# The causal mask of all attention scores moves from TensorE products to a VectorE addition in PSUM

## The chip, the core and the metric

The kernel runs on one core of a Trainium2 chip. Its time is the device time of one execution in microseconds (us). The engines are named as in the profile: PE is TensorE (PEld its weight loads), DVE is VectorE, ACT is ScalarE, POOL is GpSimd, SP is the engine that issues DMAs. PSUM (`ps` in the rows, 8 banks of 512 float32 columns on 128 partitions) is where TensorE writes its products; VectorE and ScalarE read it.

## What is computed

Two layers of a hybrid decoder over 512 positions of width 1024: a projection, three groups of token mixers (gated delta rule, sparse attention, short convolution), an output projection, and a gated FFN. The change touches the attention group alone, and of it the two branches (selected blocks and sliding window) that see, for this length, all keys up to the query's own position. Cut from the reference:

```python
p_s = masked_softmax(einsum("bqgrd,bgqkd->bgrqk", q_r, k_g) * scale, smask)   # smask: kpos <= tq
p_w = masked_softmax(einsum("bqgrd,bkgd->bgrqk", q_r, kb) * scale, wmask)
out = gt[..., 0:1] * o_c + gt[..., 1:2] * o_s + gt[..., 2:3] * o_w
...
s = jnp.where(mask, scores.astype(jnp.float32), NEG_INF)
return jnp.where(mask, jax.nn.softmax(s, axis=-1), 0.0)
```

There are 8 query heads in 4 pairs, and 4 query tiles of 128 rows. Query tile i needs the key tiles 0 to i; within key tile i only the keys on or below the diagonal count.

## The kernel before

Every engine has its own instruction stream, written out by hand in the order in which it runs, and streams wait for each other through counting semaphores. The order around the change is that order of the code; no planner moves it.

**The slots.** The attention of a layer is 24 slots. `slot_of(k)` (L413) gives head pair, branch and s = k mod 3: a slot with s = 0 handles query tiles 0 and 1, s = 1 tile 2, s = 2 tile 3, always for the two heads a = 0, 1 of a pair. Scores of a slot lie in two PSUM banks, one for each head, and the slots alternate between two such pairs of banks (`bank_of`, L422). A slot passes through these steps:

- TensorE, `scores(k)` (L883): 12 products (s = 0) or 6, at L904, then the mask. The mask is a product of the identity with a constant tile `negm` (bfloat16, 0 on and below the diagonal, -1e30 above; its second half is all -1e30), added into the same PSUM columns: four products for s = 0 (L914 for tile 0, 256 wide, so that the unused key tile 1 is masked too, and L917 for tile 1), two at L917 for s = 1 and 2. The last one raises `score`. From slot 2 on, `scores(k)` waits until the exponentials of slot k-2 have been taken, since it overwrites their banks.
- VectorE, `maximum(k)` (L1984): waits for `score`, takes one negated row maximum over the slot's scores (L1991) and raises `nmax`.
- ScalarE, `exp(k, a)` (L1369): exponentials with the row sums, for head 0, then the copy of slot k-3's transposed probabilities for head 1 out of PSUM (`evacuate`, L1381; in the rows L1168), then the exponentials of head 1.
- VectorE, `invert_sum(k)` (L1993, at L1996), which stands behind `maximum(k+1)`; then POOL, `scale_probs(k)` (L1559, at L1567).
- TensorE, `p_transpose(k)` (L921, at L930), issued behind `scores(k+3)`: transposes of the probabilities, head 0 into bank 4, head 1 into bank 5. Each waits for POOL, and for the copy of the transposed block of the slot before out of that bank: VectorE copies head 0 (`evacuate`, L1998, at L2002), ScalarE head 1.
- TensorE, `pv` (L933, at L947), for three slots at once, issued in the slots with k mod 3 = 0 from 6 to 27.

VectorE's stream in slot k is: `maximum(k)`, `invert_sum(k-1)`, `evacuate(k-3)`, and then other work that is spread over the slots: the recurrence of the delta rule (`recurrence`, L2008, part 0 at L2011 in slots 3, 6, 10, 12, part 1 at L2014 and L2018 in slots 4, 7, 11, 13), `gdn_finish` (L2023, small operations at L2026 to L2036 in slots 15 to 18), the softmax of the compressed branch (slots 2, 3, 5) and the low parts of the outputs (L2043, slots 11, 17, 19, 20, 22, 23). POOL multiplies the finished delta output in slots 18 to 20 (L1575, L1578), TensorE transposes it in slots 22 and 23 (`gdn_out`, L986, at L991). In slots 11, 17 and 23 TensorE's `cmp_pv` (L952, at L956) stands between the score products and the mask. Products of the output projection (`out_filler`, at L1003) follow slot 23, and then the output projection and the FFN.

The core of TensorE's part, with what follows in the same function left out:

```python
for i in tiles_of(s):
    c0 = 256 if i == 1 else 0
    for a in range(2):
        if i == 0:
            mm = nc.tensor.matmul(ps[:, b0 + a, 0:256], identb[:], negm[:], start=False, stop=True,
                                  skip_group_check=True)
        else:
            mm = nc.tensor.matmul(ps[:, b0 + a, c0 + i * P:c0 + (i + 1) * P], identb[:], negm[:, 0:P],
                                  start=False, stop=True, skip_group_check=True)
mm.then_inc(S["score"], 1)
```

Of the kernel before, what the change touches and what calls it, by code (L numbers as in the profile page):

```python
# [12 lines left out]
ALU = mybir.AluOpType  # L13
# [3 lines left out]
P = 128  # L17
# [11 lines left out]
N_SLOTS = 24  # L29
CMP_SLOTS = (8, 9)  # L30
RECUR_SLOTS = (3, 6, 10, 12)
OG_SLOT = 13
OUT_SLOTS = (22, 23)
RSQRT_SEED = 1597463007.0
# [49 lines left out]
def trunk(nc, A, out):  # L84
# [41 lines left out]
    with ExitStack() as ctx:  # L126
# [291 lines left out]
        def tiles_of(s):  # L418

            return ((0, 1), (2,), (3,))[s]  # L420
# [140 lines left out]
        def tensor_layer(pe, l):  # L561
# [321 lines left out]
            def scores(k):  # L883
# [15 lines left out]
                for i in tiles_of(s):  # L899
                    n, c0 = max(256, (i + 1) * P), 256 if i == 1 else 0  # L900
                    for part in range(3):
                        for a in range(2):
                            rows = slice(a * HEAD, (a + 1) * HEAD)
                            nc.tensor.matmul(ps[:, b0 + a, c0:c0 + n],  # L904
                                             hhi[rows, (p, 4 + p, p)[part], i * P:(i + 1) * P],
                                             hlo[rows, (br, br, 2 + br)[part], 0:n],
                                             start=part == 0 and i != 1, stop=False, skip_group_check=True)
                if k % 6 == 5 and k >= 11:
                    cmp_pv((k - 11) // 6)
                for i in tiles_of(s):  # L910
                    c0 = 256 if i == 1 else 0
                    for a in range(2):
# [6 lines that stand above are left out]
# [684 lines left out]
        def vector_layer(dve, chain, l):  # L1603
# [380 lines left out]
            def maximum(k):  # L1984
                s, b0, col = k % 3, bank_of(k), att_at(k)
                dve.wait_ge(*S.at("score", k + 1, l))
                if s == 0:
                    v, n = ps[:, b0:b0 + 2, :].rearrange("p a (i c) -> p (a i) c", i=2), 4
                else:
                    v, n = ps[:, b0:b0 + 2, 0:(s + 2) * P], 2  # L1990
# [190 lines left out]
```

## Time and profile before

| | us |
|---|---|
| median of 3 runs (1374.85 to 1375.87) | 1375.87 |
| the profiled execution, its own time | 1375.91 |
| its span, first to last instruction | 1373.8 |

| engine | busy us | share of the span |
|---|---|---|
| PE (products) | 1357.8 | 99% |
| PEld (weight loads) | 1145.2 | 83% |
| POOL | 617.8 | 45% |
| DVE | 616.0 | 45% |
| ACT | 507.1 | 37% |

The busy time is a sum over all stages. Products on TensorE are pipelined, and their ends are modelled, so a busy PE says little of a single stage; where TensorE waits for another engine is read from the chain of waits and from the timelines. Rows of windows show, after the stretch and its length, busy time and instruction count of PE, PEld, DVE, ACT and POOL, then the granted clock (1.00 is full), DMA share and GB/s. The 24 slots of the first layer lie between 197.9 and about 283 us, those of the second between 876.8 and about 962 us.

### The profile page before, as it was taken

What the parts mean: (1) busy time and instruction counts of PE and PEld (TensorE: products, weight loads), DVE (VectorE), ACT (ScalarE), POOL (GpSimd) and SP (SyncE); (2) the same over time, 40 slices, a digit from 0 to 9 for tenths busy, and PEclk for the clock granted to TensorE, in tenths of its full rate; (3) what the DMA queues carried; (4) which work ended last, traced back from release to release, by engine and by line L of the source; (5) the groups of instructions that cost most, each with busy time, mean ns of one, the idle gap of its engine ahead of it and who ended that gap; (6) DMA issues with size and microseconds to landing.
All of it is one profiled execution on the core that took longest, in us unless ns stands there. A gap on an engine that the chain in (4) does not pass through costs nothing.

```text
span 1373.8 us, 19068 instructions
## 1 busy us (share of the span) xinstructions
PE 1357.8 (99%) x7914; PEld 1145.2 (83%) x7914; DVE 616.0 (45%) x1006; ACT 507.1 (37%) x872; POOL 617.8 (45%) x333
## 2 busy tenths in 40 slices
PE   7999999999999999999999999999999999999999
PEld 6998987788888888888879999887888888888887
DVE  5638577723344213442165495767234442144421
ACT  5564336634322122222346542456342231132210
POOL 4458217633444434443344663276444444344442
PEclk9999999999999999999999999999999999999999
DMA  7325200124332233333222442010223322433322
GB/s 186 102 70 133 81 19 1 32 62 99 92 93 92 84 111 96 93 93 114 85 83 76 113 126 62 0 30 5 83 72 105 108 87 85 119 96 92 93 84 84
DMA packets 178566, 114.70 MB, mean 83 GB/s; under 512 B 46128, under 2 KB 161072, under 8 KB 178480
## 3 DMA queue, kind: packets, MB, share of 16 engines
q1 hardware_dynamic: 176368, 113.22, 29.3%
q8 instruction: 63, 1.03, 0.3%
q10 hardware_dynamic: 2112, 0.26, 0.1%
q14 instruction: 23, 0.19, 0.0%
HBM read 109.80 MB, written 3.67 MB: 83 GB/s over the span
## 4 chain that ended last, share of the span: by engine, by line
PE 94%; DVE 3%; POOL 1%; issue 1%; DMA 1%; SPq 0%; ACT 0%; DVEq 0%
PE ps L642 71%; PE ps L1003 6%; PE ps L752 2%; PE ps L947 2%; PE ps L930 2%; PE ps L904 2%; PE ps L627 1%; PE ps L678 1%; PE ps L956 1%; PE ps L305 1%; PE ps L732 1%; POOL arena L1567 1%; DVE att L1991 1%; PE ps L865 1%; PE ps L595 1%
## 5 line engine op out<-in xcount | busy, mean ns | idle before, releaser
L1493 POOL TENSOR_TENSOR w_lo<-w_raw,w_hi 128x2048 fp32r<-128x2048 f32 (+3 forms) x98 | 443.4, 4525 | 605.5 <-ACT w_hi L1158 548.3
L1158 ACT ACTIVATE w_hi<-w_raw 128x2048 fp32r<-128x2048 f32 (+1 forms) x100 | 188.6, 1886 | 555.8 <-PE ps L642 519.9
L642 PE MATMUL ps<-hT_hi,w_lo 128*128 128x512 f32 x928 | 231.3, 391 | 0.0
L642 PE MATMUL ps<-hT_hi,w_hi 128*128 128x512 f32 x896 | 224.3, 392 | 0.0
L642 PE MATMUL ps<-hT_lo,w_hi 128*128 128x512 f32 x896 | 222.7, 390 | 0.0
L642 PEld LDWEIGHTS ps<-hT_hi,w_lo 128*128 128x128 f32 x928 | 173.3, 188 | 35.8 <-issue 0.3
L642 PEld LDWEIGHTS ps<-hT_lo,w_hi 128*128 128x128 f32 x896 | 167.7, 188 | 35.1 <-issue 0.3
L642 PEld LDWEIGHTS ps<-hT_hi,w_hi 128*128 128x128 f32 x896 | 166.7, 188 | 34.3 <-issue 0.4
L2043 DVE TENSOR_TENSOR aT_lo<-ffn_tmp,aT_hi 128x512 fp32r<-128x512 f32 x44 | 142.0, 3227 | 30.7 <-ACT aT_hi L1168 30.7
L2109 DVE TENSOR_TENSOR ffn_tmp<-ps,ffn_tmp 128x512 f32<-128x512 f32 x44 | 30.4, 691 | 243.8 <-ACT ffn_tmp L1454 243.8
L2118 DVE SCALAR_TENSOR_TENSOR x_tok<-ps,st,x_tok 128x512 f32<-128x512 f32 x32 | 24.0, 751 | 175.4 <-PE ps L642 175.4
L642 PE MATMUL ps<-w_hi,aT_hi 128*128 128x512 f32 x352 | 95.7, 390 | 0.0
L642 PE MATMUL ps<-w_hi,aT_lo 128*128 128x512 f32 x352 | 95.4, 389 | 0.0
L642 PE MATMUL ps<-w_lo,aT_hi 128*128 128x512 f32 x352 | 95.4, 389 | 0.0
L642 PEld LDWEIGHTS ps<-w_lo,aT_hi 128*128 128x128 f32 x352 | 66.1, 188 | 13.8
L642 PEld LDWEIGHTS ps<-w_hi,aT_lo 128*128 128x128 f32 x352 | 66.1, 188 | 13.8
L642 PEld LDWEIGHTS ps<-w_hi,aT_hi 128*128 128x128 f32 x352 | 65.8, 188 | 13.5
L1991 DVE TENSOR_REDUCE att<-ps 128x4 f32<-128x1024 f32 (+2 forms) x48 | 54.3, 1132 | 25.5 <-PE ps L917 24.8
L1168 ACT ACTIVATE arena<-ps 128x512 f32<-128x512 f32 (+5 forms) x82 | 43.0, 547 | 50.4 <-PE ps L787 14.1
L1567 POOL TENSOR_SCALAR arena<-arena,att,ngt 128x128 f32<-128x128 f32 (+2 forms) x64 | 38.8, 617 | 45.4 <-DVE att L1996 44.9
L642 PE MATMUL ps<-w_hi,hT_hi 128*128 128x256 f32 (+2 forms) x320 | 47.9, 292 | 0.0
L642 PE MATMUL ps<-w_lo,hT_hi 128*128 128x256 f32 (+2 forms) x320 | 46.2, 287 | 0.0
(316 smaller groups left out, 1795.7 us busy)
## 6 DMA issues: line engine op xcount, KB each, us to landing
w_raw<-in_w_gate_up SPq DMA_DIRECT2D x88, 512.0 KB, 5.0
w_raw<-in_w_in SPq DMA_DIRECT2D x20, 1024.0 KB, 5.4
w_raw<-in_w_down SPq DMA_DIRECT2D x16, 1024.0 KB, 5.0
w_raw<-in_w_down SPq DMA_DIRECT2D x8, 768.0 KB, 4.5
w_raw<-in_w_out SPq DMA_DIRECT2D x16, 256.0 KB, 3.8
w_raw<-in_w_out SPq DMA_DIRECT2D x8, 512.0 KB, 4.8
w_raw<-in_w_in SPq DMA_DIRECT2D x2, 1120.0 KB, 5.5
w_raw<-in_w_in SPq DMA_DIRECT2D x2, 1056.0 KB, 7.0
```

Of the source, the lines that this page charges most:

```text
L642: mm = nc.tensor.matmul(out_ap, a(ab, k), b(bb, k), start=first and i == 0, stop=last and i == len(kts) - 1)
L752: mm = nc.tensor.matmul(ps[:, bank, h * P:(h + 1) * P], lhs(h), rhs(h), start=True, stop=True)
L904: nc.tensor.matmul(ps[:, b0 + a, c0:c0 + n], hhi[rows, (p, 4 + p, p)[part], i * P:(i + 1) * P], hlo[rows, (br, br, 2 + br)[part], 0:n], st ...
L930: mm = nc.tensor.transpose(ps[:, 4 + a, b * P:(b + 1) * P], prob_of(k, a, i)[:, j * P:(j + 1) * P], ident[:])
L1003: mm = nc.tensor.matmul(ps[:, OUT_BANKS[pair][t], :], mix[ab](OUT_KS[half][j])[:, t * P:(t + 1) * P], W[bb][:, j, :], start=first and part ...
L1158: nc.scalar.activation(whi[:, c % 2, 0:kt * w], raw[:, c % 2, 0:kt * w], ACT.Copy).then_inc(S["w_hi"], 1)
L1168: return nc.scalar.activation(dst, src, ACT.Copy, scale=scale)
L1493: nc.gpsimd.tensor_tensor(wlo[:, c % 2, 0:kt * w], raw[:, c % 2, 0:kt * w], whi[:, c % 2, 0:kt * w].bitcast(F32), ALU.subtract).then_inc(S ...
L1567: ins = nc.gpsimd.tensor_scalar(q, q, att[:, 1, col:col + 1], ngt[:, i, 3 * h + 1 + br:3 * h + 2 + br], ALU.mult, ALU.mult)
L1991: V.tensor_reduce(att[:, 0, col:col + n], v, AX, ALU.max, negate=True).then_inc(S["nmax"], 1)
L2043: V.tensor_tensor(dst, full, hi.bitcast(F32), ALU.subtract).then_inc(done, 1)
L2109: V.tensor_tensor(ft[:, 2 + cnt % 2, :], ps[:, ffn_bank(cnt, 1), :], ft[:, cnt % 2, :], ALU.mult).then_inc(S["up_mul"], 1)
```

## The change

`DVE_MASK_SLOT = 0` makes the new branch hold for every slot. TensorE's `scores(k)` ends with the score products; the last of them raises `score`, in slots 11, 17 and 23 ahead of `cmp_pv`. VectorE's `maximum(k)` begins with one addition of `negm` in place in PSUM, over the diagonal blocks of both heads (256 columns, or 512 for s = 0, where tiles 0 and 1 have one each), and waits for it before the maximum. For s = 0 the one maximum over 1024 columns becomes two, over 256 and 512 columns, which leave out the unused key tile of query tile 0.

```diff
+DVE_MASK_SLOT = 0
...
-                            nc.tensor.matmul(ps[:, b0 + a, c0:c0 + n],
+                            mm = nc.tensor.matmul(ps[:, b0 + a, c0:c0 + n],
                                              hhi[rows, (p, 4 + p, p)[part], i * P:(i + 1) * P],
                                              hlo[rows, (br, br, 2 + br)[part], 0:n],
-                                             start=part == 0 and i != 1, stop=False, skip_group_check=True)
+                                             start=part == 0 and i != 1, stop=part == 2 and k >= DVE_MASK_SLOT,
+                                             skip_group_check=True)
+                if k >= DVE_MASK_SLOT:
+                    mm.then_inc(S["score"], 1)
                 if k % 6 == 5 and k >= 11:
                     cmp_pv((k - 11) // 6)
+                if k >= DVE_MASK_SLOT:
+                    return
...
                 dve.wait_ge(*S.at("score", k + 1, l))
+                if k >= DVE_MASK_SLOT:
+                    if s == 0:
+                        v = ps[:, b0:b0 + 2, :].rearrange("p a (i c) -> p a i c", c=P)[:, :, 0:4:3, :]
+                        m = negm[:, 0:P].rearrange("p (a i c) -> p a i c", a=1, i=1).broadcast_to([P, 2, 2, P])
+                    else:
+                        v = ps[:, b0:b0 + 2, (s + 1) * P:(s + 2) * P]
+                        m = negm[:, 0:P].rearrange("p (a c) -> p a c", a=1).broadcast_to([P, 2, P])
+                    chain(V.tensor_tensor(v, v, m, ALU.add))
+                if s == 0 and k >= DVE_MASK_SLOT:
+                    V.tensor_reduce(att[:, 0, col:col + 4:2], ps[:, b0:b0 + 2, 0:P], AX, ALU.max, negate=True)
+                    V.tensor_reduce(att[:, 0, col + 1:col + 4:2], ps[:, b0:b0 + 2, 256:512], AX, ALU.max, negate=True
+                                    ).then_inc(S["nmax"], 1)
+                    return
```

TensorE's stream at slots 6 and 7 of a layer, before (scores at L904, mask at L914 and L917, transposes of probabilities at L930):

```order
L904 MATMUL ps<-hT_lo,hT_hi 128x256 [waits exp,qlo]
L904 MATMUL ps<-hT_lo,hT_hi 128x256 x11
L914 MATMUL ps<-negm,identb 128x256 x2
L917 MATMUL ps<-negm,identb 128x128 x2
L930 MATMUL ps<-ident,pbuf 128x128 [waits pTd,pscaled]
```

and with the change:

```order
L905 MATMUL ps<-hT_lo,hT_hi 128x256 [waits exp,qlo]
L905 MATMUL ps<-hT_lo,hT_hi 128x256 x11
L936 MATMUL ps<-ident,pbuf 128x128 [waits pTd,pscaled]
L936 MATMUL ps<-ident,pbuf 128x128 x2
L936 MATMUL ps<-ident,pbuf 128x128 [waits pTa,pscaled]
```

The four mask products are gone, and the transposes stand directly behind the scores; their waits are the same.

VectorE's stream at slots 18 to 20, before (maximum at L1991, inverse at L1996, copy out of PSUM at L2002):

```order
L1991 TENSOR_REDUCE att<-ps 128x4 [waits score,dve_chain]
L1996 RECIPROCAL att<-att 128x2 [waits exp]
L2002 COPY pbuf<-ps 128x384 [waits pv,ptr]
L2034 TENSOR_TENSOR st<-st 128x16
L2035 SCALAR_TENSOR_TENSOR st<-st 128x16 [waits dve_chain]
L2036 SCALAR_TENSOR_TENSOR st<-st 128x16 [waits dve_chain]
L1991 TENSOR_REDUCE att<-ps 128x2 [waits score]
L1996 RECIPROCAL att<-att 128x4 [waits exp]
L2002 COPY arena<-ps 128x384 [waits pv,ptr]
L2043 TENSOR_TENSOR aT_lo<-arena,aT_hi 128x512 [waits mixc_hi]
L1991 TENSOR_REDUCE att<-ps 128x2 [waits score]
```

and with the change, where the same operations carry lines 19 higher:

```order
L2000 TENSOR_TENSOR ps<-ps,negm 128x2x2x128 [waits score,dve_chain]
L2002 TENSOR_REDUCE att<-ps 128x2 [waits dve_chain]
L2003 TENSOR_REDUCE att<-ps 128x2
L2015 RECIPROCAL att<-att 128x2 [waits exp]
L2021 COPY pbuf<-ps 128x384 [waits pv,ptr]
L2053 TENSOR_TENSOR st<-st 128x16
L2054 SCALAR_TENSOR_TENSOR st<-st 128x16 [waits dve_chain]
L2055 SCALAR_TENSOR_TENSOR st<-st 128x16 [waits dve_chain]
L2000 TENSOR_TENSOR ps<-ps,negm 128x2x128 [waits score]
L2010 TENSOR_REDUCE att<-ps 128x2 [waits dve_chain]
L2015 RECIPROCAL att<-att 128x4 [waits exp]
L2021 COPY arena<-ps 128x384 [waits pv,ptr]
```

In front of each maximum stands one addition, and the maximum waits for it; the slot with s = 0 has two maxima. The rest of VectorE's stream keeps its order, and those of ScalarE and POOL are unchanged.

## Rows read from the trace of the kernel before

**Rows 1.** The page: busy time by engine; the chain that ended last, by engine.

```profile
PE 1357.8 (99%) x7914; PEld 1145.2 (83%) x7914; DVE 616.0 (45%) x1006; ACT 507.1 (37%) x872; POOL 617.8 (45%) x333
...
PE 94%; DVE 3%; POOL 1%; issue 1%; DMA 1%; SPq 0%; ACT 0%; DVEq 0%
```

**Rows 2.** Windows cut at each `pv`: length, busy us by engine, granted clock, DMA.

```profile
197.90:216.95 19.05, 18.09 (x163) 14.64 (x162) 15.61 (x29) 12.71 (x40) 9.88 (x15) 1.00 0.00 1
216.95:228.01 11.06, 11.06 (x114) 9.11 (x113) 8.51 (x19) 5.65 (x21) 8.91 (x11) 1.00 0.01 1
228.01:239.56 11.55, 11.55 (x116) 9.42 (x115) 7.00 (x17) 7.29 (x23) 8.48 (x11) 1.00 0.01 1
239.56:250.73 11.17, 10.66 (x109) 8.67 (x109) 7.91 (x16) 5.57 (x20) 6.01 (x9) 1.00 0.33 96
250.73:259.91 9.18, 9.06 (x91) 6.68 (x90) 7.38 (x19) 8.00 (x24) 4.76 (x8) 1.00 0.01 2
259.91:268.56 8.65, 8.50 (x90) 6.33 (x89) 8.16 (x16) 5.65 (x20) 6.91 (x11) 1.00 0.00 0
268.56:279.88 11.32, 11.26 (x95) 8.70 (x94) 6.17 (x12) 7.29 (x23) 8.57 (x14) 1.00 0.01 2
216.95:279.88 62.93, 62.09 (x607) 48.90 (x606) 45.13 (x94) 39.45 (x125) 43.65 (x63) 1.00 0.06 18
895.89:958.75 62.86, 62.05 (x607) 48.85 (x607) 45.00 (x94) 39.37 (x125) 43.64 (x63) 1.00 0.06 19
```

**Rows 3.** Chain that ended last, first layer: start us, us, what.

```profile
226.66 0.33 PE ps L914 x2
226.99 0.11 PE ps L917 x2
...
231.72 0.22 PE ps L917 x2
...
255.62 0.85 PE ps L956 x2
...
271.83 0.74 POOL arena L1578
...
272.61 0.66 PE ps L991 x4
```

**Rows 4.** Lines by form, 190 to 305 us: busy us, mean ns, idle before.

```profile
L1991 DVE TENSOR_REDUCE att<-ps 128x4 f32<-128x1024 f32 x8 | 9.7, 1218 | 0.7 <-PE ps L917 0.6
...
L1991 DVE TENSOR_REDUCE att<-ps 128x2 f32<-128x768 f32 x8 | 7.7, 956 | 9.8 <-PE ps L917 9.8
```

**Rows 5.** VectorE additions and products near the new one: ns min/median/max.

```profile
L2011 DVE TENSOR_TENSOR arena<-arena,ps x8: 394/415/422, 209.5 to 921.5; 128x256 f32<-128x256 f32 x8
...
L1608 DVE TENSOR_TENSOR ps<-ps,rbt x16: 698/699/700, 27.9 to 791.1; 128x512 f32<-128x512 f32 x16
```

**Rows 6.** Timeline of VectorE, slots 19 and 20: start us, us, what.

```profile
264.69 0.84 DVE L2043 TENSOR_TENSOR aT_lo<-arena,aT_hi 128x512 fp32r<-128x512 f32 x1
265.45 1.21 DVE L1991 TENSOR_REDUCE att<-ps 128x2 f32<-128x1024 f32 x1
...
266.66 0.67 DVE L2002 COPY spare<-ps 128x512 f32<-128x512 f32 x1
```

**Rows 7.** Timeline of ScalarE, slot 20.

```profile
266.70 0.69 ACT L1378 ACTIVATE spare<-ps,att 128x512 f32<-128x512 f32 x1 [0.81 <-DVE att L1991]
...
267.38 0.59 ACT L1168 ACTIVATE spare<-ps 128x512 f32<-128x512 f32 x1
```

**Rows 8.** Timeline of TensorE's weight loads, slot 21.

```profile
268.08 0.31 PEld L930 LDWEIGHTS ps<-ident,arena 128*128 128x128 f32 x3 [0.33 <-issue]
```

**Rows 9.** Timeline of TensorE's products, slots 18 and 19.

```profile
259.91 2.40 PE L947 MATMUL ps<-idle_w,arena 128*64 128x256 f32 x36
262.24 0.79 PE L904 MATMUL ps<-hT_lo,hT_hi 64*128 64x384 f32 x6
262.97 0.28 PE L917 MATMUL ps<-negm,identb 128*128 128x128 bf16 x2
```

## The prediction

> **What bounds the kernel now.** I read the page first: TensorE is busy for 99% of the span, and 94% of the chain that ended last is TensorE [rows 1]. By that alone anything taken off TensorE would be time won, and VectorE, busy for 45%, could take it. That share is a mean over stages, so I cut the attention slots of the first layer at the start of each `pv` [rows 2]. There VectorE is not at 45%: it is busy for 15.61 of 19.05 us, 8.51 of 11.06, 7.00 of 11.55, 7.91 of 11.17, 7.38 of 9.18, 8.16 of 8.65 and 6.17 of 11.32 us, together 60.7 of 82.0. The sixth round is full on VectorE and on TensorE (8.50) at once.
>
> Then I looked at who waits for whom where slots are tight. A transpose's second half needs ScalarE's copy of the block before it, and this copy stands behind the first exponential, which needs the row maximum. In slot 20 the maximum ends at 266.66 [rows 6], the exponential starts at 266.70, the copy at 267.38 for 0.59 [rows 7], and TensorE's weight loads for the second half start at 268.08, after standing still for 0.33 [rows 8]: 1.42 us from the end of the maximum. TensorE is busy nearly all of that round, but it has no slack against the maximum, and VectorE, which came to this maximum straight from other work (L2043) [rows 6], sets when it ends. The chain's last part before the output projection runs through VectorE's `gdn_finish` and POOL's products, the last of which ends at 272.57 and lets TensorE go on at 272.61 [rows 3].
>
> **What the change removes.** The mask costs TensorE 0.33 + 0.11 us in an s = 0 slot and 0.22 in the others [rows 3]. Eight rounds of three slots in a layer: 8 x (0.44 + 0.22 + 0.22) = 7.0 us, for both layers 14.1.
>
> **What it adds.** The trace has no PSUM addition with a bfloat16 operand. The nearest rows are a PSUM operand with 256 columns at 0.415 us, and 512 columns in place in PSUM at 0.699 [rows 5]; as the in-place one is no dearer per column than its like, I take 0.42 and 0.70. A dependent operation adds about 0.04 for the semaphore (the exponential starts 0.04 behind the maximum [rows 6, 7]; on one engine I take the same). A bound below is half of each, if a bfloat16 operand ran twice as fast; a bound above is the duration of the maximum that it precedes, 0.96 and 1.22 [rows 4]. The columns and the memory are those of rows 5, so I take their end. In the s = 0 slots one maximum over 1024 columns becomes two. From 1218 ns for 1024 columns and 956 for 768 [rows 4] a column costs 1.02 ns and the start 0.17 us, so 256 and 512 columns cost 0.43 and 0.70. An independent operation starts 0.08 before the end of the one before it (265.45 against 264.69 + 0.84) [rows 6], so the two take 1.06 in place of 1.22. VectorE gains per round: 0.74 - 0.16 = 0.58 for s = 0, and 0.46 twice: 1.50, for a layer 8 x 1.50 = 12.0 us. That makes 72.7 us of work in windows that last 82.0, and in the sixth round 9.7 in 8.65.
>
> The Trainium skill (VectorE: DVE Perf Modes, The DRAIN you can't avoid) says that the next operation does not start until the pipe is empty, and advises few operations. Here the start is 0.08 before the end [rows 6]. By the page's rule the split maximum would cost 0.08 more in each of 16 slots, and the sum below would be at most 1.3 us higher.
>
> **The path, step by step.** Take a round without other work, from the end of the scores with s = 1. VectorE: addition 0.46, maximum 0.96, inverse and copy 0.49, some 0.2 less than the 0.67 of the 512-column copy [rows 6], which begins as the maximum ends: 1.91. Then the slot with s = 2, whose scores are long there: 0.46 + 1.21 = 1.67. ScalarE's half exponential and copy to TensorE: 1.42. TensorE: half a transpose 0.33, `pv` 2.33 (259.91 to 262.24) [rows 9], the scores of the next s = 1 slot 0.73 (262.24 to 262.97): 3.39. The ring is 8.39 us. Without the additions and with the mask (0.22) and the wake-up behind it (0.1) the same ring is 7.79, and another one decides, through the exponentials: maximum, exponentials, scores with their 0.44 of mask, transpose, `pv`. The fifth round shows its length: 9.18 [rows 2] less the 0.85 of its compressed-branch product [rows 3] is 8.33. So a plain round gets some 0.1 us longer: what TensorE no longer does is eaten by 0.92 of additions in a row.
>
> Other VectorE work between these maxima goes straight onto the ring. I walked all slots of the first layer in this way, each with its waits:
> - Start to first `pv`: slots 4 and 5 hold the recurrence and a softmax on VectorE, which is the bound already (15.61 of 19.05 busy): +1.3.
> - Round 2: the state update in slot 7 stands before the maximum of slot 8: +0.3.
> - Round 3: VectorE has over 4 us to spare, and in slot 11 the score signal now comes ahead of the compressed-branch product: -0.7.
> - Round 4: as round 2: +0.2.
> - Round 5: five small `gdn_finish` operations between slots 16 and 17: +0.6.
> - Round 6: 8.39, with 0.76 of L2043 and about 0.8 by which `gdn_finish` in slot 18 outlasts the scores of slot 19, 9.95 against 8.65: +1.3.
> - Round 7: POOL's products start later with `gdn_finish`, and TensorE waits for them and for L2043 as before: +0.1.
>
> The sum is +3.1 us in a layer. The second layer has the same work in the same time (62.86 against 62.93 between first and last `pv`) [rows 2]: +3.1 again. Behind the last `pv` TensorE runs the output projection and FFN from its own queue, and the split weights (L1158, L1493) follow TensorE; I know of nothing there that gives the delay back, or adds to it. From the profiled execution's 1375.91, which is 0.04 over the median of the runs, 1375.9 + 6.2 = 1382.1 us, slower by 0.45%.
>
> **The rivals.**
> (a) TensorE stays the bound and VectorE swallows the additions in its idle time, 82.0 - 60.7 = 21.3 us in a layer against 12.0 added. Then up to 14.1 us are won: 1361.8. Partial forms lie between that and 1373. For it: TensorE's 99%, and rounds 2, 3 and 4, in which VectorE has 2.6 to 4.6 us to spare. Against it: the stall in front of the transposes [rows 8] and the full sixth round. It decides where the maximum ends more than about 1 us before its copy is wanted.
> (b) A draw: the loss in rounds 1, 5 and 6 is as I say, but the other four give the mask back, as round 3 does. Then a layer has 3.2 lost less 4 x 0.7 won, and the time is 1376.7, within 0.2%.
> (c) VectorE is in series everywhere, and no slot keeps TensorE's gain: all 12.0 us go on the path, 24 in all: 1399.9. If TensorE's gain counts in full against it, the difference is 5.0 in a layer, 1385.9. For it: VectorE is at 72.7 of 82.0 with waits of its own. Against it: its long waits in round 3. Dearer additions point the same way: every 0.1 us more in each costs at most 4.8 us.
> (d) The change doesn't do what it says: mask products could remain, or another engine's order change. The order of the changed program has no line with a mask product (128 fewer), 64 more VectorE operations (48 additions and 16 maxima), and as many rows as before on ScalarE and POOL; I give it nothing.
>
> The granted clock is 1.00 in each window [rows 2], also in the first, where TensorE is idle for 0.96 us; I put no loss on it.
>
> **How the numbers follow.** My forecast, slower by 1 to 5 us a layer, has 0.62; (c) has 0.10; together slower by over 0.2% 0.72. (b) has 0.16. (a) with its partial forms has 0.12. 0.2% is 2.75 us, about what a measurement can tell from no change. A walk over 24 slots can be off by some 2 us a layer; additions at the lower bound take some 0.4 off a round, 1375.7 in all, and at the upper bound they put over 1.0 on it, 1399. The range goes from 1374 (into the draw, and leaves (a) out) to 1390 (into (c)), and leaves out 2 in 10.
>
> **What would show it.** In the changed profile: L2000 near 0.42 and 0.70 us; the two maxima near 0.43 and 0.70; VectorE's busy time up by about 24 us; `pv` to `pv` near 8.4 to 10 us in rounds 5 and 6; in the chain VectorE's share up from 3% and TensorE's idle time in front of L936 in the slots. Wrong I would be if `pv` to `pv` in rounds 2, 4 and 7 fell by 0.5 us or more, if additions cost under 0.3 us, or if the change came from outside the slots.

## The result, and the profile after

The change took 1383.62 us, median of 4 runs (1382.11 to 1385.2), against 1375.87 of the kernel before (1374.85 to 1375.88, 4 runs). The ratio is 1.0056, interval [1.0044, 1.0068]: slower, by 7.7 us. Five more runs of it beside 15 of the kernel before gave 1.0056 again (e9 below). The profiled execution took 1382.11 us with a span of 1380.4.

The page of the changed kernel, busy time by engine and the chain by engine, beside [rows 1]:

```profile
PE 1348.8 (98%) x7786; PEld 1136.9 (82%) x7786; DVE 636.7 (46%) x1070; ACT 506.8 (37%) x872; POOL 618.6 (45%) x333
...
PE 90%; DVE 5%; issue 1%; DMA 1%; POOL 1%; ACT 1%; SPq 0%; DVEq 0%
```

TensorE has 9.0 us less of busy time and takes longer. What it lost in the chain (94% to 90%), VectorE gained in part (3% to 5%). The new operations by source line (ns min/median/max, first and last start, forms):

```profile
L2000 DVE TENSOR_TENSOR ps<-ps,negm x48: 420/433/700, 198.2 to 961.1; 128x256 f32<-128x256 f32 x32, 128x512 f32<-128x512 f32 x16
```

```profile
L2002 DVE TENSOR_REDUCE att<-ps x16: 423/424/425, 198.9 to 954.0; 128x2 f32<-128x256 f32 x16
```

```profile
L2003 DVE TENSOR_REDUCE att<-ps x16: 678/680/681, 199.3 to 954.3; 128x2 f32<-128x512 f32 x16
```

The windows of the first layer, cut at each `pv` of the changed kernel, answer to [rows 2]. The columns are length, then busy us (count) of TensorE, its weight loads, VectorE, ScalarE and GpSimd, granted clock, DMA share, GB/s:

```profile
197.18:217.59 20.41, 16.87 (x143) 13.48 (x143) 18.29 (x38) 12.74 (x40) 9.94 (x15) 1.00 0.00 1
217.59:229.04 11.45, 10.53 (x105) 8.65 (x104) 9.98 (x25) 5.65 (x21) 8.97 (x11) 1.00 0.00 1
229.04:240.16 11.12, 11.12 (x107) 9.00 (x106) 7.55 (x19) 7.25 (x23) 8.50 (x11) 1.00 0.01 1
240.16:251.73 11.57, 10.10 (x102) 8.22 (x101) 9.48 (x22) 5.58 (x20) 6.04 (x9) 1.00 0.32 93
251.73:261.59 9.86, 8.60 (x84) 6.23 (x83) 8.55 (x21) 8.01 (x24) 4.80 (x8) 1.00 0.00 1
261.59:271.24 9.65, 7.95 (x81) 5.84 (x81) 9.45 (x20) 5.65 (x20) 7.38 (x11) 1.00 0.01 2
271.24:282.80 11.56, 11.10 (x92) 8.55 (x91) 7.18 (x16) 7.19 (x23) 8.15 (x14) 1.00 0.00 1
```

Only the third round is still full on TensorE (11.12 of 11.12); in the others it idles for 0.5 to 3.5 us. In the sixth VectorE is busy for 9.45 of 9.65 us. The lengths add up to 85.62 us, against 81.99 before: +3.63. The second layer has 85.60, +3.61. So the profiled executions differ by 7.2 us in these rounds, where the change was made; the medians differ by 7.7, and the profiled executions by 6.2 as a whole, in the main since the changed one reached its first slot 0.7 us earlier (197.18 against 197.89).

TensorE's idle time now stands in brackets ahead of the transposes, with VectorE's copy of the block as its releaser (timeline of TensorE, slots 6 to 21):

```profile
216.50 1.16 PE L936 MATMUL ps<-ident,pbuf 128*128 128x128 f32 x6 [1.69 <-DVE idle_w L2021]
...
250.64 1.16 PE L936 MATMUL ps<-ident,arena 128*128 128x128 f32 x6 [1.35 <-DVE spare L2021]
...
270.15 1.05 PE L936 MATMUL ps<-ident,arena 128*128 128x128 f32 x5 [0.93 <-DVE spare L2021]
```

And the chain that ended last, through slots 19 and 20, has VectorE from end to end (start us, us, what), where the chain before had TensorE:

```profile
264.64 0.47 DVE st L2055
265.11 0.36 DVE ps L2000
...
265.49 0.11 DVE att L2010
...
266.53 0.44 DVE arena L2021
266.98 0.77 DVE aT_lo L2062
267.75 0.35 DVE ps L2000
...
268.12 0.05 DVE att L2010
```

L2055 is the end of `gdn_finish`, L2010 the maximum (L1991 before), L2021 the copy (L2002 before), L2062 the split that the prediction calls L2043. Both run immediately ahead of an addition on VectorE, and the addition ahead of the maximum.

### The profile page after: what moved, and what is told of

Read it like the earlier page. It is cut to its first block, busy times and chain, and to the rows that moved or that the text cites. A ratio compares the mean times of both kernels' runs of the same rounds, so it can differ in the third digit from the quotient of the medians.

```text
span 1380.4 us, 18876 instructions
## 1 busy us (share of the span) xinstructions
PE 1348.8 (98%) x7786; PEld 1136.9 (82%) x7786; DVE 636.7 (46%) x1070; ACT 506.8 (37%) x872; POOL 618.6 (45%) x333
## 4 chain that ended last, share of the span: by engine, by line
PE 90%; DVE 5%; issue 1%; DMA 1%; POOL 1%; ACT 1%; SPq 0%; DVEq 0%
PE ps L643 70%; PE ps L1009 6%; PE ps L953 2%; PE ps L753 2%; PE ps L936 2%; PE ps L905 1%; POOL w_lo L1499 1%; DVE ps L2000 1%; DVE att L2010 1%; PE ps L679 1%; DMA w_raw<-in_w_in 1%; PE ps L866 1%; PE ps L733 1%; PE ps L596 1%; DMA x_tok<-in_x 0%
## 5 line engine op out<-in xcount | busy, mean ns | idle before, releaser
L643 PE MATMUL ps<-hT_hi,w_lo 128*128 128x512 f32 x928 | 231.2, 391 | 0.0
L643 PE MATMUL ps<-hT_hi,w_hi 128*128 128x512 f32 x896 | 224.3, 392 | 0.1
L643 PE MATMUL ps<-hT_lo,w_hi 128*128 128x512 f32 x896 | 222.7, 390 | 0.0
L643 PEld LDWEIGHTS ps<-hT_hi,w_lo 128*128 128x128 f32 x928 | 173.3, 188 | 35.8 <-issue 0.3
L643 PEld LDWEIGHTS ps<-hT_lo,w_hi 128*128 128x128 f32 x896 | 167.8, 188 | 35.0 <-issue 0.3
L643 PEld LDWEIGHTS ps<-hT_hi,w_hi 128*128 128x128 f32 x896 | 166.7, 188 | 34.6 <-issue 0.4
L2062 DVE TENSOR_TENSOR aT_lo<-ffn_tmp,aT_hi 128x512 fp32r<-128x512 f32 x44 | 142.1, 3229 | 30.7 <-ACT aT_hi L1174 30.7
L643 PE MATMUL ps<-w_hi,aT_hi 128*128 128x512 f32 x352 | 95.7, 390 | 0.0
L643 PE MATMUL ps<-w_hi,aT_lo 128*128 128x512 f32 x352 | 95.4, 389 | 0.0
L643 PE MATMUL ps<-w_lo,aT_hi 128*128 128x512 f32 x352 | 95.4, 389 | 0.0
L643 PEld LDWEIGHTS ps<-w_lo,aT_hi 128*128 128x128 f32 x352 | 66.1, 188 | 13.8
L643 PEld LDWEIGHTS ps<-w_hi,aT_lo 128*128 128x128 f32 x352 | 66.1, 188 | 13.7
L643 PEld LDWEIGHTS ps<-w_hi,aT_hi 128*128 128x128 f32 x352 | 65.9, 188 | 13.5
L643 PE MATMUL ps<-w_hi,hT_hi 128*128 128x256 f32 (+2 forms) x320 | 47.9, 292 | 0.0
L643 PE MATMUL ps<-w_lo,hT_hi 128*128 128x256 f32 (+2 forms) x320 | 46.2, 287 | 0.0
L643 PE MATMUL ps<-w_hi,hT_lo 128*128 128x256 f32 (+2 forms) x320 | 46.1, 287 | 0.0
```

The source lines that it names most:

```text
L643: mm = nc.tensor.matmul(out_ap, a(ab, k), b(bb, k), start=first and i == 0, stop=last and i == len(kts) - 1)
L2062: V.tensor_tensor(dst, full, hi.bitcast(F32), ALU.subtract).then_inc(done, 1)
```

## The experiments

All ratios are against the kernel before, run beside it on the same chip. The rounds of all kernels, in us, cut at each `pv` (round 1 from the first scores), are read off the timelines of TensorE in the profiled execution. They are those of the first layer; the second has the same to 0.02, except in e4 (20.80 and 13.19 in rounds 1 and 2), e9 (20.40 and 13.12) and e6, whose first layer has 20.76, 12.57 and, in round 7, 11.74. e7 is left out, for the reason given there.

| kernel | 1 | 2 | 3 | 4 | 5 | 6 | 7 | sum |
|---|---|---|---|---|---|---|---|---|
| before | 19.06 | 11.06 | 11.55 | 11.17 | 9.18 | 8.65 | 11.32 | 81.99 |
| the change | 20.41 | 11.45 | 11.12 | 11.57 | 9.86 | 9.65 | 11.56 | 85.62 |
| e1, no mask | 18.27 | 10.98 | 11.12 | 11.09 | 8.92 | 8.43 | 11.27 | 80.08 |
| e2, both masks | 21.01 | 11.53 | 11.55 | 11.64 | 10.06 | 9.64 | 11.78 | 87.21 |
| e3, slack slots | 18.69 | 10.99 | 11.12 | 11.10 | 9.18 | 8.66 | 11.32 | 81.06 |
| e4, tight slots | 21.15 | 12.74 | 11.55 | 11.65 | 9.85 | 9.66 | 11.56 | 88.16 |
| e5, signal first | 19.07 | 11.06 | 11.89 | 11.17 | 9.14 | 8.65 | 11.66 | 82.64 |
| e6, second layer | 20.40 | 11.46 | 11.12 | 11.56 | 9.84 | 8.88 | 11.76 | 85.02 |
| e8, all three | 17.97 | 11.77 | 11.12 | 10.56 | 9.20 | 8.26 | 11.94 | 80.82 |
| e9, change again | 20.76 | 12.54 | 11.13 | 11.56 | 9.84 | 9.64 | 11.58 | 87.05 |
| e10, filler | 20.41 | 11.45 | 11.12 | 11.56 | 9.84 | 9.65 | 11.57 | 85.60 |
| e11, last state | 18.69 | 11.00 | 11.12 | 10.57 | 9.19 | 8.66 | 11.33 | 80.56 |

### The two halves of the change, each alone

**No mask on either engine.** The change without its additions:

```diff
-                if k >= DVE_MASK_SLOT:
+                if False:
                     if s == 0:
...
-                if s == 0 and k >= DVE_MASK_SLOT:
+                if s == 0:
                     V.tensor_reduce(att[:, 0, col:col + 4:2], ps[:, b0:b0 + 2, 0:P], AX, ALU.max, negate=True)
```

> Leaves out the causal mask altogether: TensorE has no mask products, VectorE no additions, so the future keys of the diagonal blocks count. The maxima are those of the change (two for s = 0). It prices TensorE's saving alone. Theory 1 (the ring of maximum, ScalarE's copy, transpose and pv has no slack in rounds 1, 5, 6, so little of TensorE's 14.1 us is won there; in rounds 2, 3, 4 most is): about 9 us faster than before, 1365 to 1369. Rival (TensorE alone is the bound, and only the additions hurt): the full 14.1 us, 1361 to 1363.

Measured: 1372.31 us (1371.12 to 1373.24, 7 runs), ratio 0.9972 [0.9962, 0.9983]. This missed: 14.1 us of products off TensorE, with nothing put in their place and VectorE a little lighter, are worth 3.6 us, where about 9 were expected. There are two reasons. The first is that the products never cost the 14.1 (slots 10 to 12 below). The second stands in the windows of rounds 2 to 4:

```profile
216.43:227.41 10.98, 10.52 (x105) 8.64 (x105) 8.36 (x21) 5.63 (x21) 8.91 (x11) 1.00 0.01 1
227.41:238.53 11.12, 11.12 (x107) 9.00 (x106) 6.56 (x16) 7.18 (x23) 8.48 (x11) 1.00 0.01 1
238.53:249.62 11.09, 10.09 (x101) 8.21 (x100) 7.84 (x18) 5.56 (x20) 6.01 (x9) 1.00 0.33 97
```

Rounds 2 and 4 give 0.08 each, although TensorE works 0.54 and 0.57 us less in them than before: the difference is idle time. In round 2 the chain that ended last runs here, from products of the recurrence through VectorE's state update to the maximum:

```profile
221.95 0.80 PE ps L988 x7
...
222.77 0.42 DVE arena L2033
223.19 0.18 DVE state L2037
```

So TensorE, busy for 11.06 of 11.06 us in this round before, had no time to win there: a ring through VectorE was just as long.

**Both masks.** The kernel before with the additions and the split maxima as well, so that the mask counts twice:

```diff
                 if s == 0:
-                    v, n = ps[:, b0:b0 + 2, :].rearrange("p a (i c) -> p (a i) c", i=2), 4
+                    w = ps[:, b0:b0 + 2, :].rearrange("p a (i c) -> p a i c", c=P)[:, :, 0:4:3, :]
+                    m = negm[:, 0:P].rearrange("p (a i c) -> p a i c", a=1, i=1).broadcast_to([P, 2, 2, P])
+                else:
+                    w = ps[:, b0:b0 + 2, (s + 1) * P:(s + 2) * P]
+                    m = negm[:, 0:P].rearrange("p (a c) -> p a c", a=1).broadcast_to([P, 2, P])
+                chain(V.tensor_tensor(w, w, m, ALU.add))
...
```

> TensorE keeps all its mask products, and VectorE does the change's additions and maxima on top (the mask is added twice). It prices VectorE's work alone. Theory 1: in the tight rounds the ring grows by the additions (0.9 to 1.5 us a round), in rounds 3 and 4 most of them are hidden: 8 us a layer, 1389 to 1394. Rival (VectorE in series everywhere, rival c of the prediction): 12 us a layer, 1399 or more. If the additions were free (rival a): 1376.

Measured: 1385.91 (1385.06 to 1386.51, 5 runs), ratio 1.0072 [1.0059, 1.0084]. This missed as well, from below (1389 to 1394 were expected): additions and maxima that the prediction put at 24 us, and that raise VectorE's busy time by 20.7 (616.0 to 636.7), cost 10.0. In the profile the rounds are 10.4 longer (5.2 in a layer), by +1.95, +0.47, 0, +0.47, +0.88, +0.99 and +0.46. Round 3 has room for all of its additions; round 4, which was expected to hide most, is 0.47 longer. The two halves alone give -3.6 and +10.0, together +6.4 against the measured 7.7.

### Where the additions cost nothing, and where they cost all

**Slack slots alone.** VectorE adds the mask in nine of the 24 slots, TensorE in the others:

```diff
-DVE_MASK_SLOT = 0
+DVE_MASK_SLOTS = (0, 1, 7, 9, 10, 11, 12, 13, 23)
...
-                if k >= DVE_MASK_SLOT:
+                if k in DVE_MASK_SLOTS:
```

> The change in slots 0, 1, 7, 9 to 13 and 23 alone, where the trace of before shows VectorE waiting for the scores before or soon after the maximum; mask products on TensorE in the 15 others. Theory 1: TensorE's savings there (5.3 us for both layers) come through and the additions hide: 2 to 5 us faster than before, 1371 to 1374. Rival (each addition costs more than its product wherever it stands): slower than before, by 9/24 of the change's 7.7 us: 1379.

Measured: 1373.51 (1372.99 to 1374.55, 11 runs), ratio 0.9983 [0.9974, 0.9992]: the time is in the expected range, but not because TensorE's 5.3 us came through; 2.4 did, and by the distances measured in slots 10 to 12 below these nine slots could give about 2.6. Its rounds 2 to 4:

```profile
215.85:226.84 10.99, 10.59 (x107) 8.73 (x106) 9.14 (x22) 5.65 (x21) 8.96 (x11) 1.00 0.01 1
226.84:237.96 11.12, 11.12 (x107) 9.00 (x106) 7.68 (x19) 7.35 (x23) 8.49 (x11) 1.00 0.01 1
237.96:249.06 11.10, 10.60 (x107) 8.59 (x107) 9.05 (x19) 5.58 (x20) 6.04 (x9) 1.00 0.35 97
```

They are as long as those of e1, in which nobody adds a mask (10.98, 11.12, 11.09), with 0.8 to 1.2 us more work on VectorE in each. In the slots of these rounds (7 and 9 to 13) the additions are wholly hidden. Slots 0, 1 and 23 are not shown one by one: round 1 is 0.37 shorter than before, and round 7 as long.

**Tight slots alone**, the other fifteen:

```diff
-DVE_MASK_SLOT = 0
+DVE_MASK_SLOTS = (2, 3, 4, 5, 6, 8, 14, 15, 16, 17, 18, 19, 20, 21, 22)
```

> The complement: the change in slots 2 to 6, 8, and 14 to 22, mask products on TensorE in slots 0, 1, 7, 9 to 13, 23. Theory 1: all of the loss and more, since the slots that gave something back are left out: 1385 to 1389. Rival (cost by the number of additions): 15/24 of 7.7 us, 1380 to 1381.

Measured: 1386.47 (1385.92 to 1388.16, 5 runs), ratio 1.0078 [1.0066, 1.0091], as expected, and more than the whole change. Its rounds 5 to 7 are those of the change (9.85, 9.66, 11.56). Its second round of 12.74 holds something else, a lower clock (below): granted 0.90 in that round, and 0.87 in the 13.19 of the second layer. If that cost what it cost in e9 (1.45 us in the first layer and 1.67 in the second), its layers of 88.16 and 88.28 would have 86.7 and 86.6, +4.6 to +4.7; this is an estimate. The slack slots' -0.9 and this make +3.7 a layer, the change's +3.63. As far as that estimate goes, the change is the sum of its slots: nine that win together, fifteen that lose together.

### One term, the early score signal

The prediction gave round 3 its -0.7 partly for the score signal coming ahead of the compressed-branch product in slot 11. The kernel before with that alone:

```diff
-                if k % 6 == 5 and k >= 11:
-                    cmp_pv((k - 11) // 6)
                 for i in tiles_of(s):
...
                 mm.then_inc(S["score"], 1)
+                if k % 6 == 5 and k >= 11:
+                    cmp_pv((k - 11) // 6)
```

> The kernel before, with one part of the change alone: in slots 11, 17 and 23 the compressed-branch product (0.85 us) stands behind the mask products and the score signal instead of between scores and mask. Theory 1: only slot 11 has a VectorE that waits for the signal (1.26 us), and the ring through it has slack in that round: within 0.5 us of before, 1375.4 to 1376.0. Rival (the early signal is what made round 3 shorter by 0.4 in the change): 0.8 us faster, 1375.0 or less.

Measured: 1377.66 (1376.56 to 1378.97, 11 runs), ratio 1.0011 [1.0002, 1.002]. This missed: the kernel is 1.7 us slower, where at most 0.1 was expected. It wins nothing, and rounds 3 and 7 get 0.34 longer. TensorE's timeline of slot 11, before (scores L904, compressed product L956, mask L917, transposes L930):

```profile
232.97 0.97 PE L904 MATMUL ps<-hT_lo,hT_hi 64*128 64x512 f32 x6
233.78 1.02 PE L956 MATMUL ps<-arena,vcr 64*128 64x512 f32 x2
234.72 0.28 PE L917 MATMUL ps<-negm,identb 128*128 128x128 bf16 x2
234.85 0.82 PE L930 MATMUL ps<-ident,spare 128*128 128x128 f32 x6
```

and with the signal first:

```profile
232.80 0.96 PE L904 MATMUL ps<-hT_lo,hT_hi 64*128 64x512 f32 x6
233.70 0.29 PE L915 MATMUL ps<-negm,identb 128*128 128x128 bf16 x2
233.91 1.12 PE L956 MATMUL ps<-arena,vcr 64*128 64x512 f32 x2
234.97 1.09 PE L930 MATMUL ps<-ident,spare 128*128 128x128 f32 x8
```

From the scores to the transposes it is 1.88 us before and 2.17 here, the same products in another order: 0.90 + 0.21 + 1.06 in place of 0.81 + 0.94 + 0.13. In the changed kernel, without the mask, the same stretch is

```profile
233.93 0.98 PE L905 MATMUL ps<-hT_lo,hT_hi 64*128 64x512 f32 x6
234.75 1.02 PE L962 MATMUL ps<-arena,vcr 64*128 64x512 f32 x2
235.70 0.87 PE L936 MATMUL ps<-ident,spare 128*128 128x128 f32 x6
```

1.77 us: TensorE saved 0.11 there, where the prediction counted 0.22.

Slot 10, with nothing between the scores and the mask, tells the same. Before:

```profile
230.93 0.79 PE L904 MATMUL ps<-hT_lo,hT_hi 64*128 64x384 f32 x6
231.65 0.29 PE L917 MATMUL ps<-negm,identb 128*128 128x128 bf16 x2
231.77 0.83 PE L930 MATMUL ps<-ident,arena 128*128 128x128 f32 x6
232.43 0.61 PE L967 MATMUL ps<-state,arena 128*128 128x128 f32 x4
```

and in the changed kernel:

```profile
231.96 0.79 PE L905 MATMUL ps<-hT_lo,hT_hi 64*128 64x384 f32 x6
232.68 0.87 PE L936 MATMUL ps<-ident,arena 128*128 128x128 f32 x6
233.39 0.61 PE L973 MATMUL ps<-state,arena 128*128 128x128 f32 x4
```

From scores to transposes 0.84 and 0.72 us, so 0.12 less; but the transposes take 0.66 before and 0.71 now, 0.05 more. In slot 12 (s = 0) the timelines give 1.25 and 0.91, 0.34 less, and 0.04 given back; in slot 11 it is 0.11, and 0.05 given back. Together (0.12 + 0.11 + 0.34) - 0.14 = 0.43 us for the round, which is exactly by how much round 3 is shorter. The prediction's 0.44 + 0.22 + 0.22 = 0.88 counted the chain's durations [rows 3], twice what the neighbours' starts moved. If the other rounds are like this one, eight rounds and two layers make 6.9 us, not 14.1, that TensorE could give at all; that is an estimate from one round.

### Moving VectorE's other work out of the way

**The two splits to slot 21**, in the changed kernel:

```diff
-                if k in (OG_SLOT + 6, OG_SLOT + 7):
-                    m = k - OG_SLOT - 6
+                for m in (0, 1) if k == OG_SLOT + 8 else ():
```

> The change, with VectorE's two L2062 operations (0.85 and 0.89 us) moved from the ends of slots 19 and 20 to the end of slot 21, behind which VectorE waits 1.4 us for scores. Same work in each layer. Theory 1 (other work between the tight maxima lies on the ring): round 6 shrinks from 9.65 us to about 8.9, round 7 grows by 0.2 at most, 0.6 to 0.9 us a layer faster than the change: 1381.8 to 1382.4 against its 1383.6. Rival (the bound is VectorE's total work, or latency that is the same): no difference from the change.

Measured: 1383.35 (1380.84 to 1384.12, 5 runs), ratio 1.0052 [1.004, 1.0065]; 1381.8 to 1382.4 were expected. Round 6 falls from 9.65 to 8.88 in both layers, 0.77 us, one split's time: the split stands in series there. Round 7 gives back 0.20. In the time as a whole this can't be told from the change. The profiled execution (1384.06) lost about 1.5 us in the first two rounds of its first layer (20.76, 12.57), with the clock granted at 0.73 and 0.70 between 217 and 223 us; what the other four lost is not on record. The mechanism is shown, the gain in the time is not.

**State updates one slot later**, with the slack slots of e3. Of the four updates the first and the last are put behind the copy of the slot after:

```diff
+                if k in (RECUR_SLOTS[0] + 2, RECUR_SLOTS[3] + 2):
+                    recurrence(RECUR_SLOTS.index(k - 2), 1)
...
-                if k - 1 in RECUR_SLOTS:
+                if k - 1 in RECUR_SLOTS[1:3]:
...
-                if k == OG_SLOT:
+                if k == OG_SLOT + 1:
```

> The slack-slot version (additions in slots 0, 1, 7, 9 to 13, 23) with the first and the last state update of the recurrence (1.5 us on VectorE each) moved behind the maximum, inverse and copy of the next slot, from the end of slots 4 and 13 to slots 5 and 14. TensorE stands still there for 0.68 and 0.50 us in that version. Theory 1: both stalls go, 0.8 to 1.2 us a layer, 1.6 to 2.4 in all: 1371.1 to 1371.9. Rival (VectorE's order does not matter, only its sum): 1373.5 as without the move.

Measured: 1372.54 us, median of seven (1371.94 to 1373.27), ratio 0.9976 [0.9965, 0.9986]; 0.6 us short of what was expected. An eighth, the profiled one, took 4762.65 us. In it TensorE is busy for 4750.0 us, and its products of 512 float32 columns (L643) last 1.10 us on the mean where they last 0.39 before, while the other engines are busy about as long as ever. Nothing about the rounds can be read there. The next run, the same with the move of e6 added, can be read.

> As the one before, and the two L2062 operations moved to the end of slot 21 as well. Theory 1: round 6 is at 8.66 us in the slack-slot version, where TensorE has no slack to give but small stalls in front of the transposes: 0.2 to 0.3 us a layer on top, 1370.5 to 1371.5. Rival: as the one before, or slower by what slot 22 waits for, up to 0.5.

Measured: 1373.19 (1372.12 to 1374.87, 11 runs), ratio 0.9982 [0.9973, 0.9991]: missed, no better than e3 alone. Against e3, the rounds say which move did what: the first update wins 0.72 in round 1 and gives back 0.78 in round 2; the last wins 0.54 in round 4 and nothing gives it back; the splits win 0.40 in round 6, and round 7 is 0.62 longer, all of it a wait for POOL's products of the delta output, in slot 22 (timeline of TensorE):

```profile
270.35 0.66 PE L997 MATMUL ps<-ident,arena 128*128 128x128 f32 x4 [0.71 <-POOL arena L1584]
```

Why only the first update's gain comes back can be read off VectorE's timelines. The first move makes the maximum of slot 6 start 1.5 us later against the `pv` in that slot, the last one that of slot 15. Behind slot 15 VectorE waits in e3 for 0.31 and 1.10 us until the maximum of slot 16, and the delay disappears in these waits. Behind slot 6 it waits for 0.73 and 0.31, less than the delay, and the chain of round 2 in e8 then runs on through another state update.

**Only the last update moved**, which is what was left of e8 as a gain:

```diff
+                if k == OG_SLOT + 1:
+                    recurrence(3, 1)
...
-                if k - 1 in RECUR_SLOTS:
+                if k - 1 in RECUR_SLOTS[:3]:
...
-                if k == OG_SLOT:
+                if k == OG_SLOT + 1:
```

> The slack-slot version with the last state update alone moved from the end of slot 13 to slot 14, behind maximum, inverse and copy. In e8_all_three round 4 fell from 11.10 to 10.56 by this move, while the first state update's move won 0.72 in round 1 and lost 0.78 in round 2. Theory 1: round 4 at 10.56, the others as in the slack-slot version, 0.54 us a layer: 1372.2 to 1372.6. Rival (what is won is given back in round 5, as it was between rounds 1 and 2): 1373.5.

Measured: 1372.31 (1372.05 to 1374.57, 11 runs), ratio 0.9977 [0.9968, 0.9986], as expected. Round 4 takes 10.57 us and is now nearly full on TensorE, busy for 10.45 of them, where before it was 10.66 of 11.17 [rows 2]. This kernel is faster than the one before and than the change, and as fast as e1, which adds no mask at all. e7, with a ratio of 0.9976, can't be told from it.

### The clock behind the stalls

e4, e6 and the change differ in their second rounds by more than their edits explain. In e4 TensorE's granted clock is 0.50 between 218 and 221 us. So the change was run again, as it is, and once with work for TensorE in its stall in slot 6: twelve transposes of a constant into a PSUM bank that is free there.

> The change itself, once more, for its spread and its granted clock, beside the next one. Theory 2 (in the two profiles e4_tight_slots and e6_mixc_to_21 TensorE ran below full clock for some us behind the stalls of slots 5 and 6, and lost 1.1 to 1.9 us each time; in the profile of the change it did not): its runs spread over 1382 to 1385, and slower ones have a mean clock below 1. Rival (the spread has another source, such as the first DMAs): the spread is there, without any relation to where the clock was granted.

Measured: 1382.63 (1382.49 to 1387.43, 5 runs), ratio 1.0056 [1.0044, 1.0069]. The profiled execution is the one of 1387.43, 5.3 us over that of the change; the four others are at 1382.49 to 1383.03. The mean clock of a whole execution does not tell them apart: it is 0.997 in the slowest, and 0.998 in the two fastest. First TensorE's stall and the windows behind it, in this execution:

```profile
217.68 1.51 PE L936 MATMUL ps<-ident,pbuf 128*128 128x128 f32 x6 [1.69 <-DVE idle_w L2021]
```

```profile
214.50:217.50 3.00, 1.49 (x17) 1.12 (x16) 2.90 (x8) 1.91 (x5) 1.86 (x4) 1.00 0.00 0
217.50:219.00 1.50, 1.29 (x6) 0.81 (x6) 1.47 (x3) 1.34 (x5) 0.84 (x2) 0.66 0.00 0
219.00:222.00 3.00, 3.00 (x29) 2.51 (x30) 2.45 (x8) 0.97 (x5) 2.48 (x2) 0.60 0.02 5
```

and the same stretches, 1.2 us earlier on the clock, in the execution of the change that stands at the top:

```profile
213.30:216.30 3.00, 1.51 (x17) 1.13 (x16) 2.90 (x8) 1.91 (x4) 1.88 (x4) 1.00 0.00 0
216.30:217.80 1.50, 1.18 (x8) 0.82 (x10) 1.47 (x3) 1.37 (x5) 0.88 (x2) 1.00 0.00 0
217.80:220.80 3.00, 3.00 (x42) 2.58 (x40) 2.60 (x9) 0.95 (x5) 2.46 (x2) 1.00 0.02 5
```

The same program, the same stall of 1.69 us and the same busy time before it: once the granted clock stays at 1.00, once it falls to 0.66 and 0.60, a mix of full speed (2.4 GHz) and half (1.2 GHz), for some 4.5 us. In them TensorE gets through 29 matmuls where it otherwise does 42. This costs 1.45 us in the first layer and 1.67 in the second (87.05 and 87.27 against 85.6), 3.1 us of the 5.3. Of the rest 1.2 us lie ahead of the slots and 1.0 between those of the two layers, at a granted clock of 1.00; their cause was not looked for.

> The change, and in slot 6, where TensorE stands still for 1.69 us, 12 transposes of a constant into bank 6, whose content the first pv overwrites: 12 x 0.11 = 1.3 us more of TensorE's work in a layer. Theory 2: TensorE has no idle stretch long enough there for the clock to fall, the times lie close together at the lower edge of the change's, 1381.5 to 1382.5, with the rounds of the change's profile unchanged (20.4, 11.45). Rival (work on TensorE costs what it lasts): 2.6 us slower than the change. If the filler is merely hidden and the clock has nothing to do with it: the same median and spread as the change, 1383 to 1384.

```diff
+                if k == 6:
+                    pe.wait_ge(*S.at("cadd", 4, l))
+                    for _ in range(12):
+                        nc.tensor.transpose(ps[:, 6, 0:P], ident[:], ident[:])
```

Measured: 1382.41 (1381.96 to 1385.26, 5 runs), ratio 1.0051 [1.0038, 1.0064]. TensorE's timeline in slot 6:

```profile
214.78 1.53 PE L1044 MATMUL ps<-ident 128*128 128x128 f32 x12
216.54 0.52 PE L936 MATMUL ps<-ident,pbuf 128*128 128x128 f32 x3 [0.22 <-DVE idle_w L2025]
```

The median is where the theory had it (1381.5 to 1382.5), the spread is not. 1.5 us of work in the stall of 1.69 leave every round as it was (the table): TensorE's time is free there, which is the change's own point turned round. No clock loss shows in its profile. Whether the filler prevents one stays open: four of its runs are between 1381.96 and 1382.57, but one is at 1385.26 with a mean clock of 0.997, as in the slowest of e9, and e9's median of 1382.63 is no different. Five runs can't tell how often it happens.

## Why the prediction was right, and where not

The forecast of 1382.1 us stands 1.5 below the measured 1383.62, with the sign, the mechanism and the place as given. The comparison term by term, a layer, in us:

| round | 1 | 2 | 3 | 4 | 5 | 6 | 7 | sum |
|---|---|---|---|---|---|---|---|---|
| predicted | +1.3 | +0.3 | -0.7 | +0.2 | +0.6 | +1.3 | +0.1 | +3.1 |
| measured | +1.35 | +0.39 | -0.43 | +0.40 | +0.68 | +1.00 | +0.24 | +3.63 |

- **What the change removes: mis-sized.** 14.1 us was twice too much; 6.9 is what TensorE can give, by the estimate from slots 10 to 12 above, and e1, with no mask at all, wins 3.6. The forecast hardly suffered, since its sum was walked on rings in which the mask stood once or not at all. The upper rival did: with 6.9 in place of 14.1 its best case is 1369.0, not 1361.8.
- **Prices of the additions: right.** The additions were taken at 0.42 and 0.70 from the nearest rows; they measured 0.429 and 0.692 on the mean. The maxima were taken at 0.43 and 0.70 and measured 0.424 and 0.680. VectorE's busy time rose by 20.7 us, not by about 24: the 24 held 48 gaps of 0.04 for the semaphore, which are no busy time, about 1.9 us; the rest, I take it, is overlap of starts, which I did not count out.
- **The path: right in length, one engine off in name.** The prediction led its ring through ScalarE's copy to the second half of the transposes, at 1.42 us from the end of the maximum. In slot 20 of the changed kernel the maximum ends at 269.34 and the second half starts at 270.79, 1.45 later. But TensorE stands still before the first half, until VectorE's own copy (L2021) ends at 270.02, and only 0.12 before the second; ScalarE's copy ends at 270.65. So the two ways are equally long to some 0.1 us, and the prediction named only one of them.
- **Overlap of independent operations: right.** The prediction took starts 0.08 before the end of the operation ahead. The changed kernel's timeline agrees with the row: an L2002 of 0.42 starts at 262.38, and L2003 at 262.72, 0.08 before its end. A dependent one starts 0.02 to 0.04 behind it, as 265.49 after the addition's end at 265.47. The prediction set this against a sentence of the Trainium skill (VectorE: DVE Perf Modes, The DRAIN you can't avoid), by which the next operation does not start until the pipe is empty. It left out that the same section adds that a next operation which is not held starts earlier, and with that the trace does not contradict the page.
- **Rounds 1, 2, 4 and 5: right.** Of the ring of 8.39 us, round 5 is the cleanest measure: 8.39 + 0.85 for the compressed product + 0.6 for `gdn_finish` makes 9.84, and it took 9.86. That round 1 hangs on slots 4 and 5 is borne out by e8, which takes 0.72 off it by moving one state update. Round 4 was 0.2 short. e1 shows that before the change, too, rounds 2 and 4 hung on the state update and not on TensorE. The prediction said this of VectorE in the changed kernel, but the expectation of e1 forgot it.
- **Round 3: right in sign, mis-sized.** -0.7 measured -0.43, the whole worth of this round's mask products, and e1 has the same 11.12. The early score signal, which the prediction named beside it, is worth nothing (e5).
- **Round 6: a term mis-sized.** 9.95 predicted, 9.65 measured. The split ahead of an addition is there with its 0.77 (e6 takes it away and gets 0.77 back). `gdn_finish` outlasts slot 19's scores by less than the 0.8 that I took: the scores end at 264.71 (263.92 + 0.79), the addition starts at 265.04, 0.33 later. With 0.33 the prediction's own sum gives 9.48, so some 0.2 of the round is not explained.
- **Round 7: wait mistaken.** +0.24 for +0.1. The prediction had TensorE wait for POOL's products, which start later, and for L2043 as before. It does not wait for POOL: it stands still for 0.46 us in slot 23, for VectorE's split (L2062, before L2043), where before it is idle for 0.06 in the whole round, and it has 0.16 less to do (11.10 for 11.26). The wait, in TensorE's timeline:

```profile
278.83 0.63 PE L997 MATMUL ps<-ident,arena 128*128 128x128 f32 x4 [0.46 <-DVE aT_lo L2062]
```

- **Outside the slots** the prediction put nothing, which holds: +7.2 in the rounds of the two layers, and the profiled execution is 6.2 us over that of before, since its attention started 0.7 us earlier and its time holds 0.4 less outside the span (1.7 against 2.1). That its 1382.11 is the predicted 1382.1 is therefore chance: two errors of a half us in a layer, and a start that was early by as much.
- **The clock: wrong in part.** That the granted clock is 1.00 and no loss is to be put on it holds for the profiled execution of the change and fails in that of e9. The profile of before shows no such loss in these rounds, nor do those of e1, e3, e8 and e11, all with smaller stalls: in the first window TensorE is idle for 0.96 us before and 3.54 in the change. Taking the two layers of each profile by themselves, the clock fell in five of the eight whose first window holds 3.5 to 3.8 us of TensorE's idle time (the change none of two, e4 two, e6 one, e9 two), and in none of the sixteen with 2.6 us or less (before, e1, e2, e3, e5, e8, e10, e11). That the stalls open the way to it fits all of these, and no run separates them from what else e4, e6, e9 and the change have in common. The loss explains 3.1 us of the 1387.43 of e9. Of the 2.9 by which e4's 1386.47 is above the change, 1.9 are the slack slots' gain, which e4 leaves out (2 x 0.93); the clock can have the rest.

The rivals. (a), TensorE bound and 1361.8, is refuted by e1: with no additions to pay for, the time is 1372.3; its partial forms, up to 1373, are refuted by e2, in which the additions cost 10.0. (c), series everywhere, is refuted by e2 and e3: 10.0 of 24 us are in series, and in the slots of rounds 2 to 4 that e3 changes none is. (b), a draw in which rounds 2, 4 and 7 win as round 3 does, fails on the state update; but e3 shows that it was only a choice of slots away. (d) did not arise.

## What to carry over

Where TensorE is busy all of a round, ask what it would wait for if it had less to do: here taking the mask products away with no substitute won 3.6 us, because a ring through another engine was nearly as long, and they were worth about 6.9 and not the 14.1 of their recorded durations: count the distance between the starts of their neighbours. Work moved to a less busy engine is free only in those stages where that engine waits, and costs its whole duration where it stands ahead of the operation that releases the bound; so move it slot by slot, as e3 and e11 do (1373.5 and 1372.3), not for all slots at once (1383.6). A delay that is moved within such a ring comes back in the next round, unless the engine has a wait there that is as long as the delay (e8 against e11).

## What was unexpected on the chip

- One program, two clocks: behind stalls of TensorE of the same length the granted clock fell to 0.50 to 0.73 over some 3 to 6 us in some executions and not in others. The 36 matmuls of the first `pv` start within 2.1 us at full clock and within 3.2 in e9, and each occurrence there costs 1.5 to 1.7 us. What decides it between two executions whose records agree to 0.02 us is open.
- Products with recorded durations of 0.29 us moved their neighbours by 0.11 or 0.12, and the order of the same products mattered by 0.29 us (slot 11, e5): the two bfloat16 ones take 0.13 behind the wide pair and 0.21 ahead of it, and the scores and the wide pair take 0.09 and 0.12 more.
- In stalls of TensorE twelve additional transposes cost nothing (e10).
- One execution of e7 took 4762.65 us, 3.5 times as long as its seven others: TensorE's products of 512 float32 columns lasted 1.10 us on the mean in place of 0.39, with a granted clock of 1.00, and the busy time of the other engines hardly changed (VectorE 623.7 us, ScalarE 516.9, GpSimd 607.5). The cause is open.
